# A two-block forward pass: the convolution branch finished ahead of the forget gates, and first halves of the last projection moved between the recurrence's last levels and its values

## What is computed

```python
# mixer of the second block (heads of 128, 4 of them; C = 512 channels per branch)
p = h @ w_in
# branch 1, "hyena": three groups of 512 channels
u = short_conv(p[..., :1536]); v, x1, x2 = split(u, 3)
z = x1 * long_conv(v, hf[0]);  y = x2 * long_conv(z, hf[1])       # y = x2 * (h2 * (x1 * (h1 * v)))
# branch 2, "hgrn": query, input, two forget gates (one a direction), output gate
q, i, zf, zb, g = split(p[..., 1536:], 5)
q = silu(q) * 128**-0.5 ;  f = lb + (1 - lb) * sigmoid(z) ;  k = 1 - f
S_t = diag(f_t) S_{t-1} + k_t v_t^T ;  o_t = S_t^T q_t             # both directions, from states of a context
o = rmsnorm(o, hg_norm_g) * silu(g)
mix = concat([rmsnorm(y, hy_norm_g), o]) @ w_out
x = x + g1 * mix
# then: rmsnorm, router, 16 experts of 2048 hidden features, 32 tokens each (about 400 MB of weights)
```

## Time and profile before

| | |
|---|---|
| profiled execution, its own time | 1672.56 us |
| its span (first to last instruction) | 1670.7 us |
| median of the three runs | 1673.34 us |
| TensorE busy | 1277.7 us, 76% of the span |
| VectorE / ScalarE / GpSimd busy | 389.3 / 218.7 / 51.3 us |
| data moved | 545.13 MB, mean 326 GB/s |
| mean granted TensorE clock | 0.894 of full speed |

### The profile page before, as it was taken

One profiled execution on the slowest core, in us unless ns is written; L12 is line 12 of the kernel. 1 busy time (PEld: TensorE's weight loads), 2 busy tenths in 40 slices (PEclk: granted clock), 3 DMA queues, 4 the chain that ended last, 5 costly groups with the idle time before them and its releaser, 6 DMA issues.

```text
span 1670.7 us, 17088 instructions
## 1 busy us (share of the span) xinstructions
PE 1277.7 (76%) x7202; PEld 708.1 (42%) x7202; DVE 389.3 (23%) x782; ACT 218.7 (13%) x427; POOL 51.3 (3%) x91
## 2 busy tenths in 40 slices
PE   5999999999999998988565656476556656656664
PEld 3766678888888877862111111111111111111111
DVE  3577644454032546531000000000000000000001
ACT  2323412122202241120000000000000000000001
POOL 1100000000000012000000000000000000000000
PEclk9999999999999999998888887778887778887787
DMA  9787959666544544558999999999999999999995
GB/s 357 199 197 278 314 176 325 213 230 218 195 152 148 160 132 149 220 214 370 428 427 428 428 427 428 427 429 427 427 428 428 428 428 427 428 427 428 429 428 253
DMA packets 109838, 545.13 MB, mean 326 GB/s; under 512 B 5891, under 2 KB 73252, under 8 KB 78980
## 3 DMA queue, kind: packets, MB, share of 16 engines
q1 hardware_dynamic: 104572, 524.31, 79.6%
q0 software_dynamic: 3184, 16.86, 2.7%
q10 hardware_dynamic: 2008, 2.85, 0.5%
HBM read 539.79 MB, written 4.19 MB: 326 GB/s over the span
## 4 chain that ended last, share of the span: by engine, by line
DMA 48%; PE 44%; DVE 5%; issue 1%; ACT 1%; SPq 0%; DVEq 0%
DMA tok<-in_exp_w_dram 33%; PE L L1564 12%; DMA ring<-in_exp_w_dram 8%; PE L L1789 6%; DMA arena<-in_exp_w_dram 6%; PE L L1758 4%; PE X L1995 4%; PE X L1730 2%; PE L L1906 2%; DMA ring<-in_w_ada_dram 2%; PE L L1698 2%; PE X L2021 1%; PE L L1575 1%; PE L L1507 1%; PE L L2032 1%
## 5 line engine op out<-in xcount | busy, mean ns | idle before, releaser
L1995 PE MATMUL X<-arena,HR 128*32 128x512 f32 x1040 | 159.7, 747 | 100.7 <-DMA arena<-in_exp_w_dram 90.7
L1564 PE MATMUL L<-tok,ring 128*128 128x256 f32 x960 | 212.4, 383 | 2.0 <-ACT tok L600 1.6
L1564 PEld LDWEIGHTS L<-tok,ring 128*128 128x128 f32 x960 | 183.1, 192 | 34.3 <-issue 9.5
L1995 PE MATMUL X<-ring,HR 128*32 128x512 f32 x816 | 127.1, 752 | 72.1 <-DMA ring<-in_exp_w_dram 65.8
L2021 PE MATMUL X<-arena,HI 128*32 128x512 f32 x512 | 90.2, 842 | 53.9 <-DMA arena<-in_exp_w_dram 48.1
L1414 DVE TENSOR_TENSOR HR<-HR,X 128x512 f32<-128x512 f32 x16 | 11.0, 687 | 502.3 <-ACT HR L853 502.3
L1995 PEld LDWEIGHTS X<-arena,HR 128*32 128x32 f32 x1040 | 32.5, 125 | 218.1 <-DMA arena<-in_exp_w_dram 142.7
L1789 PE MATMUL L<-tok,ring 128*128 128x256 f32 x448 | 99.4, 379 | 0.0
L1995 PEld LDWEIGHTS X<-ring,HR 128*32 128x32 f32 x816 | 25.3, 123 | 162.6 <-DMA ring<-in_exp_w_dram 107.2
L1789 PEld LDWEIGHTS L<-tok,ring 128*128 128x128 f32 x448 | 84.4, 190 | 13.5 <-issue 2.8
L2021 PE MATMUL X<-ring,HI 128*32 128x512 f32 x400 | 62.9, 759 | 35.0 <-DMA ring<-in_exp_w_dram 32.2
(11 more groups left out here) (370 smaller groups left out, 1315.4 us busy)
## 6 DMA issues: line engine op xcount, KB each, us to landing
arena<-in_exp_w_dram SPq DMA_DIRECT2D x97, 2048.0 KB, 45.6
ring<-in_exp_w_dram SPq DMA_DIRECT2D x76, 2048.0 KB, 45.7
tok<-in_exp_w_dram SPq DMA_DIRECT2D x19, 2048.0 KB, 46.7
ring<-in_w_in_dram SPq DMA_DIRECT2D x34, 1024.0 KB, 5.4
ring<-in_w_ada_dram SPq DMA_DIRECT2D x24, 1024.0 KB, 9.0
ring<-in_w_up_dram SPq DMA_DIRECT2D x22, 1024.0 KB, 7.0
arena<-in_ada_w_dram POOLq DMA_DIRECT2D x13, 1024.0 KB, 6.2
ring<-in_ada_w_dram SPq DMA_DIRECT2D x11, 1024.0 KB, 5.1
```

The source lines that it names most:

```text
L1564: last = MM(L[:, j % 4, m * T:m * T + T], w[:, k, m * P:m * P + P], src(k), start=(k == 0), stop=(k == KT - 1))
L1995: last = MM(X[CAP * j:CAP * j + CAP, w, :], xe[:, k % 2, k // 2, :], mslot(g, u)[:, j * 512:j * 512 + 512], start=(k == 0), stop=(k == KT ...
```

## The change

1. In `WIN2` the last two hyena units (4 and 5) come before the four forget units; `accumulators()` follows.
2. On TensorE `unit("hy", 4)` stands in front of the second `forward_dft`. `unit("hy", 5)` and the last two `hyena_turn` stand among the first forget units. The second `inverse_dft` is behind forget unit 1 instead of forget unit 3. The transposes of the hyena branch (`y_turned`) move from behind the values into forget unit 3.
3. On VectorE the whole end of the hyena branch, up to `hyena_done`, comes before the first instruction of the recurrence. ScalarE's square root of that branch moves between `forget(1)` and `forget(2)`.
4. `gram` has another fill. `gram(0)` and `gram(1)` stand together in output-gate unit 0, and the last two stand in and behind the input units. `GRAM_BANK` alternates from the start.
5. The parts of the last projection that need only the hyena branch move ahead: unit 0 between `gram(7)` and `gram(8)`, half of unit 1 between `gram(8)` and the values, and the rest between the values and the transposes of the recurrence, with half of unit 3 behind those.
6. `yTh` (the turned hyena result) moves into `HR`, `ksum` to arena 12. SP's second pair waits for `gram(0)` instead of the last `hyena_turn`.

```diff
-WIN2 = (0, 1, 2, 3, 6, 7, 10, 11, 12, 13, 4, 5, 14, 15, 8, 9)
+WIN2 = (0, 1, 2, 3, 6, 7, 4, 5, 10, 11, 12, 13, 14, 15, 8, 9)
-GRAM_BANK = (2, 2, 2, 0, 2, 0, 2, 0, 2)
+GRAM_BANK = (2, 0, 2, 0, 2, 0, 2, 0, 2)
...
-            sp.wait_ge(S["hynat_done"], 6)
+            sp.wait_ge(S["gram_done"], 1)
             expert_pair(1)
...
             natural(3)
+            taps(4)
+            odd_parts(1)
+            taps(5)
+            natural(4)
             forget(0)
-            odd_parts(1)
-            for i in range(1, 4):
-                forget(i)
-            taps(4)
-            natural(4)
-            taps(5)
             natural(5)
+            forget(1)
+            reached(act, "hy_inv")
+            A(hyr, hyr, ACT.Sqrt).then_inc(S["hy_rstd"], 1)
+            forget(2)
+            forget(3)
...
             gated(0, znat, "z_ready")
+            short_conv(4)
             spectra(1)
...
             short_conv(5)
-            level(2)
             gated(1, ynat, "y_nat")
...
             inverse_dft(0)
-            unit("f", 0)
+            unit("hy", 4)
             pe.wait_ge(S["z_ready"], 1)
             forward_dft(1, lambda t: znat[:, t, :])
-            for i in range(1, 4):
-                unit("f", i)
+            unit("hy", 5)
+            hyena_turn(4)
+            unit("f", 0)
+            hyena_turn(5)
+            unit("f", 1)
             inverse_dft(1)
-            half("hy", 4, 0)
+            unit("f", 2)
+            half("f", 3, 0)
+            reached(pe, "y_normed")
...
+            half("f", 3, 1)
+            half("g", 0, 0)
+            reached(pe, "hyena_done")
             gram(0)
-            half("hy", 4, 1)
             gram(1)
...
+            half("g", 0, 1)
+            for x, (name, i) in enumerate((("g", 1), ("i", 0))):
                 half(name, i, 0)
+                gram(2 + 2 * x)
+                half(name, i, 1)
                 gram(3 + 2 * x)
...
+            half("i", 1, 0)
+            gram(6)
+            half("i", 1, 1)
+            gram(7)
+            wout2_part(0, LOW)
+            gram(8)
+            wout2_part(1, LOW, (0,))
             pe.wait_ge(S["tree_ready"], NG)
...
+            wout2_part(1, LOW, (1,))
+            wout2_part(2, LOW)
+            wout2_part(3, LOW, (0,))
+            reached(pe, "o_normed")
...
+            wout2_part(3, LOW, (1,))
             reached(pe, "hgrn_ready")
```

More of the change, by code:

```diff
@@ L116, in accumulators @@
         j += [("hy", "dve"), ("hynat", "act")]
-    j += [("q", "act")] * 2 + [("hynat", "act")] + [("f", "act")] * 4
-    j += [("hy", "dve")] * 2 + [("hynat", "act")] * 2 + [("g", "act")] * 2 + [("i", "act")] * 2
+    j += [("q", "act")] * 2 + [("hynat", "act")] + [("hy", "dve")] * 2
+    j += [("hynat", "act"), ("f", "act")] * 2 + [("f", "act")] * 2 + [("g", "act")] * 2 + [("i", "act")] * 2
     j += [("wout2", "dve")] * 4 + [("xnat", "act")] * 4
@@ L824, in _ @@
                           ACT.Copy).then_inc(S["cross_copied"], 1)
-            reached(act, "hy_inv")
-            A(hyr, hyr, ACT.Sqrt).then_inc(S["hy_rstd"], 1)
             reached(act, "hgrn_done")
@@ L1342, in _ @@
             done(last, "hyena_done")
+            out_of_bank(dve, "q", 1)
+            dve.wait_ge(S["lat_gates"], 4)
+            dve.wait_ge(S["masks_landed"], 16)
+            V.tensor_tensor(flat(ksum), flat(uA[0]), flat(uB), ALU.add)
+            V.tensor_tensor(flat(vT[:, 0, :, :]), flat(qT), flat(fT[:, 1, :, :]), ALU.mult)
+            done(V.tensor_tensor(flat(vT[:, 1, :, :]), flat(qT), flat(fT[:, 0, :, :]), ALU.mult), "tree_ready")
+            gather(0)
+            dve.wait_ge(S["tree_ready"], 1)
+            for n in range(1, NL + 1):
+                level(n)
+                gather(n)
+            dve.wait_ge(S["gram_done"], NG)
+            done(climb(P, fT, None, vT), "tree_ready")
             reached(dve, "o_sq")
@@ L1841, in gram, with wout2_part @@
                 last.then_inc(S["gram_done"], 1)
+            def wout2_part(i, ks, ms=(0, 1)):
+                n, j = upos[("wout2", i)], pos["wout2"][i]
+                landed(pe, n)
+                if ks[0] == 0:
+                    lin_free(pe, j)
+                w = slot(n).rearrange("p (k n) -> p k n", k=KT)
+                for m in ms:
+                    for k in ks:
+                        last = MM(L[:, j % 4, m * T:m * T + T], w[:, k, m * P:m * P + P], yTh[:, k, :] if k < HG else yTg[:, k - HG, :],
+                                  start=(k == 0 and m == 0), stop=(k == KT - 1), skip_group_check=True)
+                if ks[-1] == KT - 1:
+                    last.then_inc(S["unit_done"], 1)
+            LOW, HIGH = range(HG), range(HG, KT)
             unit("hy", 0)
@@ L1859, in _ @@
             inverse_dft(0)
-            unit("f", 0)
+            unit("hy", 4)
             pe.wait_ge(S["z_ready"], 1)
             forward_dft(1, lambda t: znat[:, t, :])
-            for i in range(1, 4):
-                unit("f", i)
-            inverse_dft(1)
-            half("hy", 4, 0)
+            unit("hy", 5)
[3 more added lines that the diff above has]
+            unit("f", 1)
+            inverse_dft(1)
+            unit("f", 2)
+            half("f", 3, 0)
+            reached(pe, "y_normed")
+            for c in range(HG):
+                for t in range(TT):
+                    last = nc.tensor.transpose(X[:, 2 + c // 2, (c % 2) * T + t * P:(c % 2) * T + t * P + P], ynat[:, t, c * P:c * P + P], ident)
+            last.then_inc(S["y_turned"], 1)
+            half("f", 3, 1)
+            half("g", 0, 0)
+            reached(pe, "hyena_done")
             gram(0)
-            half("hy", 4, 1)
             gram(1)
[L1870 to L1875, removed]
+            half("g", 0, 1)
+            for x, (name, i) in enumerate((("g", 1), ("i", 0))):
                 half(name, i, 0)
+                gram(2 + 2 * x)
+                half(name, i, 1)
                 gram(3 + 2 * x)
-                half(name, i, 1)
-                gram(4 + 2 * x)
-            unit("i", 1)
+            half("i", 1, 0)
[5 more added lines that the diff above has]
+            wout2_part(1, LOW, (0,))
             pe.wait_ge(S["tree_ready"], NG)
@@ L1892, in _ @@
             last.then_inc(S["hgrn_done"], 1)
-            reached(pe, "y_normed")
-            for c in range(HG):
-                for t in range(TT):
[L1896 to L1918, removed]
+            wout2_part(1, LOW, (1,))
+            wout2_part(2, LOW)
+            wout2_part(3, LOW, (0,))
+            reached(pe, "o_normed")
+            for h in range(HG):
+                for t in range(TT):
+                    last = nc.tensor.transpose(X[:, 2 + h // 2, (h % 2) * T + t * P:(h % 2) * T + t * P + P], onat[:, t, h * P:h * P + P], ident)
+            last.then_inc(S["o_turned"], 1)
+            wout2_part(3, LOW, (1,))
             reached(pe, "hgrn_ready")
@@ L1942, in _ @@
             pe.wait_ge(S["router_gained"], 1)
-            wout2_part(0, range(HG, KT))
+            wout2_part(0, HIGH)
             MM(BIASB, ones, bsb, start=True, stop=True).then_inc(S["bias_done"], 1)
@@ L1946, in _ @@
             for i in range(1, 4):
-                wout2_part(i, range(HG, KT))
+                wout2_part(i, HIGH)
                 router_part(i - 1)
```

2 lines of the change are left out of this document (1 added, 1 removed).

## The result

| | before | after |
|---|---|---|
| median of 20 runs | 1673.24 us (1670.01 to 1674.67) | 1675.31 us (1673.32 to 1676.51) |
| ratio of the runs, 95% interval | | 1.0017 (1.0011 to 1.0023) |
| profiled execution / its span | 1672.56 / 1670.7 us | 1673.98 / 1672.2 us |

The change costs 2.1 us, 0.12%. That is inside the 0.2% called no change, and with twenty runs on each side it is still clearly above zero. The forecast was 1675.0 us.

What follows compares the result with a forecast made beforehand. TensorE's work before pair 10, which starts a DMA-bound stream, was taken to bound the kernel. Order 0.7 plus clock 1.7 gave 2.4 us on 1672.56: 1675.0 us, range 1671.0 to 1679.5.

Steps and rivals of the forecast that it cites:

- What bounds the kernel: TensorE's work and waits before the experts set when pair 10 starts the DMA-bound stream; moving that moment moves the end equally.
- Wait A: At the last hyena_turn, TensorE waits 4.3 us for VectorE's short_conv(5), with forget 1 and all the rest queued behind.
- Wait B: At gram(0), TensorE waits 4.3 us instead of 0.88 for the chain of gate and products after forget 3.
- The wait ahead of tiles 4 to 7: Before tiles 4 to 7 of the last projection: a wait of 1.1 us, with their start at 720.2 us.
- The order's own cost: New order up to tiles 4 to 7: 720.2 against 719.5 us, +0.7 us, between -0.5 and +1.4.
- What costs nothing: ScalarE's extra table loads and root, VectorE's earlier hyena end, and SP's later pairs (landed by 715 us) add no time.
- The clock term: TensorE's granted clock falls behind one of the two 4.3 us waits, costing 1.7 us; the old 3.29 us wait cost nothing.
- Both waits drop the clock: Rival: clock falls at forget 1 and at the grams, 4.0 us more in all, 1676.6 us (1681.5 at most); chance 0.20.
- The router runs at full clock: Rival: shifted waits spare the router's 10 us at 0.51 clock, saving 1.8 us, giving 1671.5 us; chance 0.10.
- The third rival: Old waits go and one new one does not come, short_conv(5) or the gates being sooner: 1669.0 us; chance 0.06.

Runs made afterwards that it cites:

- experiment 8: Changed kernel with both long waits covered, all of unit 3 behind the recurrence's transposes, and six useless matmuls in the router's 3.07 us wait: 1661.33 us.
- experiment 1: Changed kernel with the second half of output-gate unit 0 moved from behind gram(1) to ahead of gram(0): 1669.96 us, ratio 0.9984 to the kernel before.
- experiment 2: Changed kernel with the last hyena_turn moved behind forget unit 1 instead of ahead of it: 1668.65 us, ratio 0.998 to the kernel before.
- experiment 9: Changed kernel with the four units of tiles 0 to 3 of the last projection put behind the values again: 1681.73 us, ratio 1.0050 to the kernel before.

## Why the prediction was right

**What bounds the kernel** held in every profile. Pair 10 starts a stream of 900.1 to 900.6 us, and what TensorE loses before it, in waits or in slow work behind them, is lost to the whole.

**Wait A** was put at 4.3 us, released by short_conv(5): 4.38. **Wait B** at 4.3, released by the products: 4.18. **The wait ahead of tiles 4 to 7** at 1.1: 1.14. No other was foretold above 0.3, and there is none. Forget 3, the hyena norm and the seven levels came as reckoned. The order's own cost, 0.7 us, measured 0.6 in the profiles with the waits filled and 0.2 to 0.3 at the medians, which are less certain.

**What costs nothing** held. The two more table loads fell into ScalarE's waits, and the three pairs that go out at gram(8)'s end (703.5 us) had landed long before the experts' first matmul (755.2): the DMA engines' share was 0.96 in the 5 us up to 720 and 0.44 in the next 5.

**The clock term** came out near its size for a partly wrong reason. The step read "that it happens at one of the two waits" at 1.7 us, on top of a kernel before that loses none. In the profile of after it falls behind both waits, 4.3 us in all, and filling them wins 3.5 to 3.9 at the median. But the kernel before, whose 3.29 us wait I had read as costing nothing, loses about 1.75 at its own median. The difference, 1.8 to 2.1, is close to 1.7 because the two errors cancel. The waits and the order were reckoned; that this term came out right was luck. What failed is the reading of one execution: the row with the clock at 1.00 was one of two outcomes of the same wait.

**The rivals.** "Both waits drop the clock" named the right mechanism at the right places. Its time of 1676.6 us was too long because the same mechanism also burdens the kernel before. The rule of the page "TensorE: Matmul & The Clock Gate" of the Trainium skill (section "Why this matters for your kernels"), no idle gaps between bursts, was the better guide than the one row of 3.29 us. The traces agree with it behind both new waits (9.39 us instead of 7.07, and 3.53 instead of 2.05), and in part behind the old one of 3.29 us, which two of four profiles show followed by a fall. "The router runs at full clock" did not happen here, though the low stretch was shorter (two of the windows behind the router: 0.60 and 0.54 over 8 us, against 0.51 over 10), and experiment 8 puts its price of 1.8 us at about 2.0. The third rival is out: spectra and the chain from forget 3 to gram(0) took what their rows said, and both new waits came.

```profile
752.00:756.00 4.00, 2.45 (x22) 0.81 (x22) 1.71 (x4) 1.67 (x2) 0.00 (x0) 0.60 0.40 168
756.00:760.00 4.00, 4.00 (x27) 0.97 (x23) 1.63 (x3) 0.00 (x0) 0.57 (x2) 0.54 0.17 33
```

**Where the expected gain went.** The change removes all six old waits, 8.5 us. It spends 9.7 on three new ones. For wait A, VectorE has 15.7 us of spectra and 1.7 of short convolution, begun 1.3 us behind the end of the forward transform (603.45 against 602.13), and TensorE has 14.3 us of work over them. For wait B, one half unit is left over a chain of 7.8. Moving one turn removes the first, and moving one half unit all but 0.73 us of the second, which shows that the idea of the change was sound and its filling was not.

## What to carry to other kernels

When work is reordered around a chain, write down for each wait that goes what stood over the chain that remains; here one turn and one half unit in other places turned +0.12% into -0.42%. In this kernel a wait of 4.2 to 4.4 us inside dense work cost its length and 1.4 to 3.0 us of lost clock on top, in all six places where a profile has one (the changed kernel and experiments 1, 2 and 9), and one of 3.29 us cost 2.7 to 2.8 in two of four. Where nothing useful can cover such a wait, useless matmuls in it won the clock back. One profile does not show whether a wait costs the clock: compare medians, or take several profiles of the same kernel.

## What the runs showed of the hardware that I had not expected

The same wait of 3.29 us, in the same kernel, left the granted clock at 1.00 in two executions and was followed by a stretch at the lower level (1.2 GHz) in two others. Even a wait of 2.72 us between dense matmuls was followed by a fall (experiment 9). Nine useless matmuls in each of two waits, which shorten nothing, made the whole kernel 3.5 to 3.9 us faster, and with six in the router the median fell by another 2.0 us.
